# Two hybrid layers on one core: eight modulation columns moved out of the attention, and VectorE copies one head's transposes

## The chip, the core and the metric

The kernel runs on one core of one Trainium2 chip. The core has a matrix engine (TensorE, "PE" in the profile, its weight loads "PEld"), VectorE ("DVE"), ScalarE ("ACT"), GpSimd ("POOL") and SyncE ("SP"), which here only issues loads. Matrix results land in PSUM, eight banks of 2 KB per partition; everything else is in SBUF. The metric is the time of one execution on the device in microseconds; the number quoted is the median of the runs.

## The reference, cut to what matters

Two layers run over 128 context tokens and 512 latent tokens of width 1024. The part of a layer that this change touches:

```python
def _modulation(cond, ada_w, ada_b):          # 6 x 1024 = 48 columns of 128 outputs
    m = jax.nn.silu(cond) @ ada_w + ada_b
    return jnp.split(m[:, None, :], 6, axis=-1)

def _layer(x, cond, mixer, ...):
    sh1, sc1, ga1, sh2, sc2, ga2 = _modulation(cond, ada_w, ada_b)
    h = _rmsnorm(x, g_pre_mix) * (1.0 + sc1) + sh1
    mixed, side = mixer(_split_proj(h, w_in))      # retention heads beside attention heads
    x = x + ga1 * _rmsnorm(mixed @ w_out, g_post_mix)
    h = _rmsnorm(x, g_pre_ffn) * (1.0 + sc2) + sh2
    x = x + ga2 * _rmsnorm(_conv_ffn(h, w_up, conv_w, conv_b, w_down), g_post_ffn)
```

The attention heads of the latent tokens (8 heads, a neighbourhood window with a bias, and 128 cached context keys) do per block of 128 queries: scores, plus bias, row maximum, exponential, row sum, and the product with the values. Only `ga1, sh2, sc2, ga2`, which are needed after the mixer, are modulation columns that this change moves.

## The kernel before, in words

All products are float32 made of three passes with operands split in a high and a low part. A weight tile of 128 x 1024 arrives by DMA in `raw`, a ring of four slots; ScalarE writes its high part to `w_hi` (split_hi, L778) and VectorE the rest to `w_lo` (split_lo, L1354), which also frees the slot. `w_hi` and `w_lo` are rings of four tiles too: tile g is split as soon as the matrix engine is done with tile g-4.

One stream of tiles per layer feeds the ring. Its order is written out by hand in `ORDER`: "w" is a weight tile, "a" a modulation column, which is also a tile of 128 x 1024. VectorE alone works a column: `ada_first` (L1365) multiplies it with the first condition vector and sums, `ada_second` (L1371) does so with the second, and only that one frees the slot. `stream_ada` and `stream_in` give the place of a tile in the stream. SyncE issues a load as soon as the slot it needs is free, strictly in stream order.

VectorE's order is the order of its code, and each engine works strictly in order. Columns 16 to 47 ("column 0" of the stream below is number 16) are scattered between the weight tiles. The input projection has seven blocks of four tiles: weight tiles 0 to 19 are blocks 0 to 4, done token tile by token tile; 20 to 27 are blocks 5 and 6, done column by column, with `kq_evac` on ScalarE turning the results into keys and queries. The retention heads run in between: `chunk_state`, `decay_queries`, `weigh_scores` and `centre` on VectorE prepare what the matrix engine takes next (`retention_block`, `retention`). Tiles 28 to 35 are the output projection.

The attention is a loop of 20 units (`PAIRS`: four head pairs with four query blocks each, then four units for the context tokens), each with two heads e = 0, 1. It is a pipeline over steps i, written out for four engines:

- PE, step i: `na_scores(i)` into banks 0 and 1 or 2 and 3; `na_transposes(i-1)`, the exponentials of head e to bank `NA_T[e]`, which is 4 or 5; `na_values(i-2)`; after every fourth unit `na_outputs`, the reciprocal row sums spread over the rows. Steps 1 to 4 also hold `mix_transposes` of the retention result.
- DVE, step i: `na_weigh(i)` (L1600, bias and maximum; L1596 for the context units), `mix_low` in steps 2 to 5, `split_lo(31)` in step 5, then from step 5 to 20 one half of a modulation column, then for a finished group the reciprocal, a copy of the result out of PSUM (L1891), one step later the product (L1895) and after it the low part (L1904).
- ACT, step i: for e = 0, 1: `exponentials(i, e)` (L1158), then `copy_transposed(i-1, e)` (L1166), which takes the transposed exponentials from bank 4 or 5 to `pt`.

The semaphores between them: `na_s` scores done, `na_m` maximum done, `na_e` exponential done, `na_t` transposed, `na_p` copied, `na_av` values done. `na_transposes(u)` waits for the exponential and for the copy that empties its bank; `na_values(u)` waits for both copies of the unit.

Of the kernel before, what the change touches and what calls it, by code (L numbers as in the profile page):

```python
# [24 lines left out]
P = 128  # L25
# [70 lines left out]

ORDER = ("wwww" "wwww" "waawaaww" "wwaawwaa" "wwww" "wwawawaaa" "wwaawaawwaawww" "aaaaaaaa" "waawaawaw")
W_POS = [i for i, kind in enumerate(ORDER) if kind == "w"]
# [69 lines left out]
def build(nc, t):  # L168
    with ExitStack() as ctx:
# [204 lines left out]
        na_t = counted("na_t", 2 * NPU)  # L374
        na_p = counted("na_p", 2 * NPU)
        na_av = counted("na_av", NPU)
# [388 lines left out]
        def _(act):  # L765
# [324 lines left out]
            for layer in range(DEPTH):  # L1090
# [77 lines left out]
                for i in range(NPU + 3):  # L1168
                    for e in range(2):
                        if i < NPU:  # L1170
                            exponentials(i, e)
                        if 1 <= i < NPU + 1:
                            copy_transposed(i - 1, e)
                    if i == 0:
# [174 lines left out]
        def _(dve):  # L1349
# [183 lines left out]
            def retention_block(layer):  # L1533

                split_lo(16, layer)
                chunk_state(1, layer)
                split_lo(17, layer)
                decay_queries(0, layer)
                chunk_state(2, layer)
                split_lo(18, layer)  # L1540
                chunk_state(3, layer)
                weigh_scores(0, layer)
                decay_queries(1, layer)
                split_lo(19, layer)
                weigh_scores(1, layer)

            def retention(layer):

                for c in range(3):
                    split_lo(20 + c, layer)  # L1550
                    centre(c, layer)
                    weigh_scores(c + 2, layer)
                    if c < 2:
                        decay_queries(c + 2, layer)
                    if c:
                        ada(ADA_FIRST + 7 + c, layer)
                split_lo(23, layer)
                centre(3, layer)
                for col in range(ADA_FIRST + 10, ADA_FIRST + 13):
                    ada(col, layer)  # L1560
# [24 lines left out]
            def na_weigh(i, layer):  # L1585
# [7 lines left out]
                for e in range(2):  # L1593
# [4 lines left out]
                    else:  # L1598
                        c0 = keys_of(jb)[0]
                        dve.tensor_tensor_reduce(sp[:, i % 2, e, 0:n], src[:, 0:n], bias[:, 2 * g + e, c0:c0 + n],  # L1600
                                                 -1.0, BIG, ALU.add, ALU.min, nmax[:, i % 2, e:e + 1]).then_inc(na_m, 1)

            def group_sums(layer):
# [224 lines left out]
            for layer in range(DEPTH):  # L1828
# [25 lines left out]

                for q in (0, 2):
                    split_lo(12 + q, layer)
                    split_lo(13 + q, layer)
                    ada(ADA_FIRST + q + 4, layer)
                    ada(ADA_FIRST + q + 5, layer)
                retention_block(layer)  # L1860
# [3 lines left out]
                for g in range(26, 31):  # L1864
                    if g in (26, 27, 29):
                        col = ADA_FIRST + 13 + 2 * (g - 26 - g // 29)
                        ada(col, layer)
# [5 lines left out]
                for i in range(NPU + 3):  # L1873
# [4 lines left out]
                    if i == 5:  # L1878
                        split_lo(31, layer)
                    if 5 <= i < 21:  # L1880
                        (ada_first if i % 2 else ada_second)(ADA_FIRST + 19 + (i - 5) // 2, layer)
                    if i == 14:
# [201 lines left out]
        def _(pe):  # L2084
# [289 lines left out]
            def na_transposes(u, layer):  # L2374
                for e in range(2):
                    pe.wait_ge(na_e, at(na_e, layer, 2 * u + e + 1))
                    if u >= 1:
                        pe.wait_ge(na_p, at(na_p, layer, 2 * u - 1 + e))
                    for i, (c0, p0, n, tile) in enumerate(spans_of(PAIRS[u])):
# [3 lines left out]
            def na_values(u, layer):  # L2383
                g, jb = PAIRS[u]
                pe.wait_ge(na_p, at(na_p, layer, 2 * u + 2))
                if jb == 0 and g >= 2:
# [405 lines left out]
```

## Time and profile before

| what | value |
|---|---|
| median of 3 runs | 1602.45 us (1602.03 to 1604.36) |
| span of the profiled execution | 1601.0 us |
| PE busy | 1575.8 us, 98% |
| DVE busy | 1275.6 us, 80% |
| ACT busy | 794.1 us, 50% |
| POOL busy | 379.2 us, 24% |
| attention loop of layer 0 / layer 1 | about 264 to 316 us / 1045 to 1096 us |

The profiled execution has no time of its own in the list of runs; its span is 1.45 us under their median. Busy times of PE are modelled, and a stretched instruction counts as busy.

### The profile page before, as it was taken

What the parts mean: (1) busy time and instruction counts of PE and PEld (TensorE: products, weight loads), DVE (VectorE), ACT (ScalarE), POOL (GpSimd) and SP (SyncE); (2) the same over time, 40 slices, a digit from 0 to 9 for tenths busy, and PEclk for the clock granted to TensorE, in tenths of its full rate; (3) what the DMA queues carried; (4) which work ended last, traced back from release to release, by engine and by line L of the source; (5) the groups of instructions that cost most, each with busy time, mean ns of one, the idle gap of its engine ahead of it and who ended that gap; (6) DMA issues with size and microseconds to landing.
All of it is one profiled execution on the core that took longest, in us unless ns stands there. A gap on an engine that the chain in (4) does not pass through costs nothing.

```text
span 1601.0 us, 28310 instructions
## 1 busy us (share of the span) xinstructions
PE 1575.8 (98%) x9688; PEld 1389.2 (87%) x9688; DVE 1275.6 (80%) x2255; ACT 794.1 (50%) x1483; POOL 379.2 (24%) x302
## 2 busy tenths in 40 slices
PE   8999999999999999999999999999999999999998
PEld 6788898689999999888878889967899999998886
DVE  7876677968999999966669556987689999998575
ACT  5433235638655565533383323274766565563333
POOL 0031033001455455200000400700035455541000
PEclk9999999999999999999999999999999999999999
DMA  9343265361222222454414414736312222335451
GB/s 369 122 132 111 74 222 179 95 168 55 66 81 89 79 92 79 148 168 158 152 40 145 138 54 134 260 107 146 79 64 82 80 91 79 92 92 178 125 184 66
DMA packets 65494, 195.04 MB, mean 122 GB/s; under 512 B 15361, under 2 KB 16769, under 8 KB 65153
## 3 DMA queue, kind: packets, MB, share of 16 engines
q1 hardware_dynamic: 50114, 175.54, 35.1%
q10 hardware_dynamic: 15296, 18.39, 3.5%
q8 instruction: 53, 0.87, 0.3%
q14 instruction: 31, 0.25, 0.1%
HBM read 187.05 MB, written 6.85 MB: 121 GB/s over the span
## 4 chain that ended last, share of the span: by engine, by line
PE 84%; DVE 7%; issue 2%; ACT 2%; DMA 1%; ACTq 1%; DVEq 0%; SPq 0%
PE bank L2087 14%; PE bank L2088 13%; PE bank L2089 13%; PE bank L2597 10%; PE bank L2599 10%; PE bank L2598 10%; DMA raw<-in_stream 1%; PE bank L2393 1%; PE bank L2457 1%; PE bank L2455 1%; PE bank L2453 1%; PE bank L2380 1%; PE bank L2109 1%; DVE w_lo L1354 1%; PE bank L2277 1%
## 5 line engine op out<-in xcount | busy, mean ns | idle before, releaser
L778 ACT ACTIVATE w_hi<-raw 128x1024 fp32r<-128x1024 f32 (+1 forms) x120 | 123.1, 1029 | 389.0 <-PE bank L2089 325.1
L1354 DVE TENSOR_TENSOR w_lo<-raw,w_hi 128x1024 fp32r<-128x1024 f32 (+1 forms) x128 | 156.3, 1228 | 162.4 <-ACT w_hi L778 162.2
L2087 PE MATMUL bank<-w_hi,aT_lo 128*128 128x512 f32 x520 | 210.5, 405 | 2.1 <-DVE aT_lo L1787 2.0
L2088 PE MATMUL bank<-w_lo,aT_hi 128*128 128x512 f32 x520 | 206.0, 396 | 0.0
L2089 PE MATMUL bank<-w_hi,aT_hi 128*128 128x512 f32 x520 | 205.6, 395 | 0.0
L2597 PE MATMUL bank<-aT_hi,w_lo 128*128 128x322 f32 x640 | 199.8, 312 | 4.5 <-DVE u L1953 4.5
L2598 PE MATMUL bank<-aT_lo,w_hi 128*128 128x322 f32 x640 | 199.4, 312 | 0.0
L2599 PE MATMUL bank<-aT_hi,w_hi 128*128 128x322 f32 x640 | 198.6, 310 | 0.0
L1252 ACT ACTIVATE w_hi<-raw 128x512 fp32r<-128x512 f32 x200 | 117.8, 627 | 105.8 <-POOL raw L660 105.8
L2087 PE MATMUL bank<-w_hi,m_lo 128*128 128x512 f32 x400 | 158.5, 396 | 0.0
L2088 PE MATMUL bank<-w_lo,m_hi 128*128 128x512 f32 x400 | 157.3, 393 | 0.0
L2089 PE MATMUL bank<-w_hi,m_hi 128*128 128x512 f32 x400 | 157.2, 393 | 0.0
L1942 DVE TENSOR_TENSOR w_lo<-raw,w_hi 128x512 fp32r<-128x512 f32 x200 | 140.7, 734 | 0.0
L2597 PEld LDWEIGHTS bank<-aT_hi,w_lo 128*128 128x128 f32 x640 | 120.7, 189 | 6.0 <-DVE u L1953 5.0
L2598 PEld LDWEIGHTS bank<-aT_lo,w_hi 128*128 128x128 f32 x640 | 121.3, 190 | 0.0
L2599 PEld LDWEIGHTS bank<-aT_hi,w_hi 128*128 128x128 f32 x640 | 121.3, 190 | 0.0
L2087 PEld LDWEIGHTS bank<-w_hi,aT_lo 128*128 128x128 f32 x520 | 98.2, 189 | 26.5 <-DVE aT_lo L1787 3.4
L2089 PEld LDWEIGHTS bank<-w_hi,aT_hi 128*128 128x128 f32 x520 | 98.4, 189 | 23.3
L2088 PEld LDWEIGHTS bank<-w_lo,aT_hi 128*128 128x128 f32 x520 | 98.4, 189 | 20.8
L649 POOL TENSOR_TENSOR raw<-raw 128x512 f32<-128x512 f32 x40 | 52.6, 1316 | 258.6 <-DVE bank L1983 137.4
L639 POOL TENSOR_TENSOR bias<-bias,masks 128x192 f32<-128x192 f32 (+1 forms) x48 | 59.1, 1269 | 198.0 <-DMA bias<-in_bias 198.0
L2599 PE MATMUL bank<-s_hi,w_hi 128*128 128x322 f32 x320 | 99.8, 312 | 0.0
(287 smaller groups left out, 3865.9 us busy)
## 6 DMA issues: line engine op xcount, KB each, us to landing
raw<-in_stream SPq DMA_DIRECT2D x304, 512.0 KB, 3.6
lead<-in_lead SPq DMA_DIRECT2D x16, 512.0 KB, 10.6
bias<-in_bias ACTq DMA_DIRECT2D x8, 896.0 KB, 10.3
na_v<-vn ACTq DMA_DIRECT2D x2, 1280.0 KB, 5.6
x<-in_xs SPq DMA_DIRECT2D x4, 512.0 KB, 12.4
vt<-na_v ACTq DMA_DIRECT2D x16, 128.0 KB
gb_mix<-gates ACTq DMA_DIRECT2D x2, 1024.0 KB, 6.2
gb_ffn<-gates ACTq DMA_DIRECT2D x8, 256.0 KB, 4.5
```

What stands on the lines that cost most here:

```text
L639: i_ = pool.tensor_tensor(part, part, masks[:, m0 * CG:(m0 + n) * CG].rearrange("p (g c) -> p g c", c=CG).unsqueeze(2) .to_broadcast([P, n ...
L649: pool.tensor_tensor(g_, g_, a_, ALU.subtract).then_inc(t1_done, 1)
L778: act.activation(w_hi[:, g % 4, 0:n], raw[:, s % 4, 0:n], ACT.Copy).then_inc(hi_done, 1)
L1252: act.activation(block_of(w_hi, n), block_source(n, e), ACT.Copy).then_inc(blk_hi, 1)
L1354: dve.tensor_tensor(w_lo[:, g % 4, 0:n], raw[:, s % 4, 0:n], w_hi[:, g % 4, 0:n].bitcast(F32), ALU.subtract).then_inc(raw_free[s % 4], 1)
L1942: i_ = dve.tensor_tensor(block_of(w_lo, n), block_source(n, e), block_of(w_hi, n).bitcast(F32), ALU.subtract)
L2087: pe.matmul(out, ll, rh, start=start, stop=False)
L2088: pe.matmul(out, lh, rl, start=False, stop=False)
L2089: return pe.matmul(out, lh, rh, start=False, stop=stop)
L2597: pe.matmul(out, wl, rhs_hi[:, k, :], start=k == 0, stop=False)
L2598: pe.matmul(out, wh, rhs_lo[:, k, :], start=False, stop=False)
L2599: i_ = pe.matmul(out, wh, rhs_hi[:, k, :], start=False, stop=k == HP - 1)
```

## The change

Three parts.

1. `ORDER`: the eight columns that stood together behind tile 31 ("aaaaaaaa") are gone from there, and every column moves forward. The stretch for block 3 (tiles 12 to 15) has eight columns instead of four, one column stands behind tile 16, two ahead of tile 20, and one more ahead of tile 23. Every tile from 24 to 31 stands exactly eight places later than before.
2. VectorE's code follows: after each of tiles 12 to 15 two columns; column 12 in `retention_block`; columns 13 and 14 at the start of `retention`; column 17 ahead of tile 23. In the attention loop no column is left.
3. ScalarE's loop keeps `copy_transposed` for e = 0 only. VectorE gets a function of the same name for e = 1, called in step i behind `na_weigh(i)`, `mix_low` and `split_lo(31)` and ahead of the group's reciprocal. It counts on a new semaphore `na_q`; `na_transposes` of head 1 waits for `na_q` in place of `na_p`, and `na_values` waits for both.

```diff
@@ -94,7 +94,7 @@
 
 
 
-ORDER = ("wwww" "wwww" "waawaaww" "wwaawwaa" "wwww" "wwawawaaa" "wwaawaawwaawww" "aaaaaaaa" "waawaawaw")
+ORDER = ("wwww" "wwww" "waawaaww" "waawaawaawaa" "wawwwaa" "wwawaawaaa" "wwaawaawwaawww" "waawaawaw")
 W_POS = [i for i, kind in enumerate(ORDER) if kind == "w"]
 A_POS = [i for i, kind in enumerate(ORDER) if kind == "a"]
 assert len(W_POS) == G_IN + G_OUT and len(A_POS) == ADA - ADA_FIRST
@@ -372,7 +372,8 @@
         na_m = counted("na_m", 2 * NPU)
         na_e = counted("na_e", 2 * NPU)
         na_t = counted("na_t", 2 * NPU)
-        na_p = counted("na_p", 2 * NPU)
+        na_p = counted("na_p", NPU)
+        na_q = counted("na_q", NPU)
         na_av = counted("na_av", NPU)
         na_r = counted("na_r", GROUPS)
         na_c = counted("na_c", GROUPS)
@@ -1166,11 +1167,12 @@
                     act.activation(pt[:, u % 2, e, 0:n], bank[NA_T[e]][:, 0:n], ACT.Copy).then_inc(na_p, 1)
 
                 for i in range(NPU + 3):
-                    for e in range(2):
-                        if i < NPU:
-                            exponentials(i, e)
-                        if 1 <= i < NPU + 1:
-                            copy_transposed(i - 1, e)
+                    if i < NPU:
+                        exponentials(i, 0)
+                    if 1 <= i < NPU + 1:
+                        copy_transposed(i - 1, 0)
+                    if i < NPU:
+                        exponentials(i, 1)
                     if i == 0:
                         kq_evac(NB_IN - 1, 3, layer)
                     if 1 <= i <= 4:
@@ -1534,6 +1536,7 @@
 
                 split_lo(16, layer)
                 chunk_state(1, layer)
+                ada(ADA_FIRST + 12, layer)
                 split_lo(17, layer)
                 decay_queries(0, layer)
                 chunk_state(2, layer)
@@ -1546,6 +1549,8 @@
 
             def retention(layer):
 
+                ada(ADA_FIRST + 13, layer)
+                ada(ADA_FIRST + 14, layer)
                 for c in range(3):
                     split_lo(20 + c, layer)
                     centre(c, layer)
@@ -1553,10 +1558,11 @@
                     if c < 2:
                         decay_queries(c + 2, layer)
                     if c:
-                        ada(ADA_FIRST + 7 + c, layer)
+                        ada(ADA_FIRST + 14 + c, layer)
+                ada(ADA_FIRST + 17, layer)
                 split_lo(23, layer)
                 centre(3, layer)
-                for col in range(ADA_FIRST + 10, ADA_FIRST + 13):
+                for col in range(ADA_FIRST + 18, ADA_FIRST + 21):
                     ada(col, layer)
                 centre(NC, layer)
                 group_sums(layer)
@@ -1599,6 +1605,13 @@
                         c0 = keys_of(jb)[0]
                         dve.tensor_tensor_reduce(sp[:, i % 2, e, 0:n], src[:, 0:n], bias[:, 2 * g + e, c0:c0 + n],
                                                  -1.0, BIG, ALU.add, ALU.min, nmax[:, i % 2, e:e + 1]).then_inc(na_m, 1)
+
+            def copy_transposed(u, layer):
+                n = P * len(spans_of(PAIRS[u]))
+                dve.wait_ge(na_t, at(na_t, layer, 2 * u + 2))
+                if u >= 2:
+                    dve.wait_ge(na_av, at(na_av, layer, u - 1))
+                dve.tensor_copy(pt[:, u % 2, 1, 0:n], bank[NA_T[1]][:, 0:n]).then_inc(na_q, 1)
 
             def group_sums(layer):
 
@@ -1852,18 +1865,17 @@
                 rotate(1, range(NT), layer)
                 split_lo(11, layer)
 
-                for q in (0, 2):
+                for q in range(4):
                     split_lo(12 + q, layer)
-                    split_lo(13 + q, layer)
-                    ada(ADA_FIRST + q + 4, layer)
-                    ada(ADA_FIRST + q + 5, layer)
+                    ada(ADA_FIRST + 2 * q + 4, layer)
+                    ada(ADA_FIRST + 2 * q + 5, layer)
                 retention_block(layer)
                 retention(layer)
                 split_lo(25, layer)
                 group_norm(layer)
                 for g in range(26, 31):
                     if g in (26, 27, 29):
-                        col = ADA_FIRST + 13 + 2 * (g - 26 - g // 29)
+                        col = ADA_FIRST + 21 + 2 * (g - 26 - g // 29)
                         ada(col, layer)
                         ada(col + 1, layer)
                     split_lo(g, layer)
@@ -1877,8 +1889,8 @@
                         mix_low((0, 1) if i == 2 else (i - 1,), layer)
                     if i == 5:
                         split_lo(31, layer)
-                    if 5 <= i < 21:
-                        (ada_first if i % 2 else ada_second)(ADA_FIRST + 19 + (i - 5) // 2, layer)
+                    if 1 <= i < NPU + 1:
+                        copy_transposed(i - 1, layer)
                     if i == 14:
                         dve.wait_ge(*freed(stream_ada(ADA_MIX - 1), layer))
                         times_gain(4 * KD, C_GF, 1.0, layer).then_inc(mod_done, 1)
@@ -2375,14 +2387,16 @@
                 for e in range(2):
                     pe.wait_ge(na_e, at(na_e, layer, 2 * u + e + 1))
                     if u >= 1:
-                        pe.wait_ge(na_p, at(na_p, layer, 2 * u - 1 + e))
+                        copied = na_q if e else na_p
+                        pe.wait_ge(copied, at(copied, layer, u))
                     for i, (c0, p0, n, tile) in enumerate(spans_of(PAIRS[u])):
                         i_ = pe.transpose(bank[NA_T[e]][:, i * P:(i + 1) * P], sp[:, u % 2, e, c0 - p0:c0 - p0 + P], ident[:])
                     i_.then_inc(na_t, 1)
 
             def na_values(u, layer):
                 g, jb = PAIRS[u]
-                pe.wait_ge(na_p, at(na_p, layer, 2 * u + 2))
+                pe.wait_ge(na_p, at(na_p, layer, u + 1))
+                pe.wait_ge(na_q, at(na_q, layer, u + 1))
                 if jb == 0 and g >= 2:
                     pe.wait_ge(na_n, at(na_n, layer, g - 1))
                 spans = spans_of(PAIRS[u])
```

VectorE in layer 0 from the split of tile 16 to that of tile 18 (L1354; `ada_first` is L1365, `ada_second` L1371, states L1514 and L1519, decayed queries L1501). Before:

```order
L1354 TENSOR_TENSOR w_lo<-raw,w_hi 128x1024
L1514 TENSOR_TENSOR sst<-st0,cdec 64x512 x2
L1519 TENSOR_TENSOR sst<-bank1,sst 64x512 x2
L1354 TENSOR_TENSOR w_lo<-raw,w_hi 128x1024
L1501 TENSOR_TENSOR qf<-qT,qexp 64x4x128 x4
L1514 TENSOR_TENSOR sst<-sst,cdec 64x512 x2
L1519 TENSOR_TENSOR sst<-bank2,sst 64x512 x2
```

After (every line number from here on is two or more higher):

```order
L1356 TENSOR_TENSOR w_lo<-raw,w_hi 128x1024
L1516 TENSOR_TENSOR sst<-st0,cdec 64x512 x2
L1521 TENSOR_TENSOR sst<-bank1,sst 64x512 x2
L1367 ISA ada_sq,mod<-raw,cond,par 128x1024
L1367 ISA mod 128x1
L1373 ISA raw,mod<-raw,cond,par 128x1024
L1373 ISA mod 128x1
L1356 TENSOR_TENSOR w_lo<-raw,w_hi 128x1024
L1503 TENSOR_TENSOR qf<-qT,qexp 64x4x128 x4
L1516 TENSOR_TENSOR sst<-sst,cdec 64x512 x2
L1521 TENSOR_TENSOR sst<-bank2,sst 64x512 x2
```

Column 12 now stands between the first state and tile 17.

VectorE in the attention loop from the end of step 5 to step 7 (L1354 splits tile 31, L1889 and L1891 are the reciprocal and the copy of the first group, L1600 `na_weigh`, L1895 the product). Before:

```order
L1354 TENSOR_TENSOR w_lo<-raw,w_hi 128x1024
L1365 ISA ada_sq,mod<-raw,cond,par 128x1024
L1365 ISA mod 128x1
L1889 RECIPROCAL rec<-esum 128x8
L1891 COPY nao<-bank6 128x512
L1600 ISA sp,nmax<-bank0,bias 128x384
L1600 ISA nmax 128x1
L1600 ISA sp,nmax<-bank1,bias 128x384
L1600 ISA nmax 128x1
L1371 ISA raw,mod<-raw,cond,par 128x1024
L1371 ISA mod 128x1
L1895 TENSOR_TENSOR nao<-nao,bank6 128x512
```

After (L1614 is the new copy, L1606 `na_weigh`, L1903 the group's copy, L1907 the product):

```order
L1356 TENSOR_TENSOR w_lo<-raw,w_hi 128x1024
L1614 COPY pt<-bank5 128x384
L1901 RECIPROCAL rec<-esum 128x8
L1903 COPY nao<-bank6 128x512
L1606 ISA sp,nmax<-bank0,bias 128x384
L1606 ISA nmax 128x1
L1606 ISA sp,nmax<-bank1,bias 128x384
L1606 ISA nmax 128x1
L1614 COPY pt<-bank5 128x384
L1907 TENSOR_TENSOR nao<-nao,bank6 128x512
```

Each half of a column has gone, and a copy from bank 5 stands ahead of the group's work.

The matrix engine in step 5, transposes of unit 4 and values of unit 3 (L2380, L2393), with what each waits for. Before:

```order
L2380 MATMUL bank4<-ident,sp 128x128 [waits na_p,na_e]
L2380 MATMUL bank4<-ident,sp 128x128 x2
L2380 MATMUL bank5<-ident,sp 128x128 [waits na_p,na_e]
L2380 MATMUL bank5<-ident,sp 128x128 x2
L2393 MATMUL bank6<-pt,ctx_v 64x128 [waits na_p]
L2393 MATMUL bank6<-pt,ctx_v 64x128
L2393 MATMUL bank6<-pt,vt 64x128 x4
```

After (L2393 and L2407):

```order
L2393 MATMUL bank4<-ident,sp 128x128 [waits na_p,na_e]
L2393 MATMUL bank4<-ident,sp 128x128 x2
L2393 MATMUL bank5<-ident,sp 128x128 [waits na_q,na_e]
L2393 MATMUL bank5<-ident,sp 128x128 x2
L2407 MATMUL bank6<-pt,ctx_v 64x128 [waits na_q,na_p]
L2407 MATMUL bank6<-pt,ctx_v 64x128
L2407 MATMUL bank6<-pt,vt 64x128 x4
```

The order is the same; the values' first product waits for two semaphores instead of one.

## Rows read from the trace of the kernel before

**Rows 1.** Page, part 1: busy time, share and instructions of each engine.

```profile
PE 1575.8 (98%) x9688; PEld 1389.2 (87%) x9688; DVE 1275.6 (80%) x2255; ACT 794.1 (50%) x1483; POOL 379.2 (24%) x302
```

**Rows 2.** Stretches: us, busy (x instructions) of PE, PEld, DVE, ACT, POOL; PEclk, DMA share, GB/s.

```profile
101.50:133.00 31.50, 31.50 (x157) 25.54 (x158) 16.86 (x20) 13.04 (x24) 19.38 (x12) 1.00 0.40 122
...
168.00:200.00 32.00, 32.00 (x258) 26.33 (x254) 22.14 (x34) 7.70 (x11) 0.00 (x0) 1.00 0.25 74
...
279.00:316.00 37.00, 35.90 (x387) 25.53 (x386) 36.07 (x95) 26.80 (x86) 0.00 (x0) 1.00 0.36 101
...
1058.00:1096.00 38.00, 36.90 (x400) 26.16 (x398) 37.07 (x97) 27.92 (x88) 0.00 (x0) 1.00 0.32 98
```

**Rows 3.** Waits, attention of layer 0 (262 to 316): us, times, longest.

```profile
PE bank L2393 <- DVE aT_lo L1582: 1.0, 1, 1.0
...
PE bank L2380 <- ACT pt L1166: 0.5, 2, 0.3
...
PE bank L2404 <- DVE nao L1891: 0.4, 1, 0.4
...
PEld bank L2393 <- issue: 4.0, 24, 0.2
```

**Rows 4.** Order of time, PE, attention: start, us, engine, instruction, [idle before <- releaser].

```profile
276.39 0.49 PE L2369 MATMUL bank<-ctx_kT,qT 64*128 64x128 f32 x4
...
288.70 0.49 PE L2369 MATMUL bank<-ctx_kT,qT 64*128 64x128 f32 x4
...
295.61 0.87 PE L2380 MATMUL bank<-ident,sp 128*128 128x128 f32 x6
...
299.63 0.49 PE L2369 MATMUL bank<-ctx_kT,qT 64*128 64x128 f32 x4
...
300.49 1.03 PE L2380 MATMUL bank<-ident,sp 128*128 128x128 f32 x6
...
308.68 0.55 PE L2380 MATMUL bank<-ident,sp 128*128 128x128 f32 x3
...
309.41 0.52 PE L2380 MATMUL bank<-ident,sp 128*128 128x128 f32 x3 [0.19 <-ACT pt L1166]
...
311.09 0.66 PE L2380 MATMUL bank<-ident,sp 128*128 128x128 f32 x2
...
313.06 0.44 PE L2380 MATMUL bank<-ident,sp 128*128 128x128 f32 x2
```

**Rows 5.** Order of time, DVE, steps 5 and 6 of the loop.

```profile
278.96 1.21 DVE L1354 TENSOR_TENSOR w_lo<-raw,w_hi 128x1024 fp32r<-128x1024 f32 x1
...
280.09 1.28 DVE L1365 CUSTOM_DVE_ANT_0 ada_sq<-raw,cond,par 128x1024 f32<-128x1024 f32 x1
...
281.41 0.64 DVE L1891 COPY nao<-bank 128x512 f32<-128x512 f32 x1
...
281.96 0.54 DVE L1600 CUSTOM_DVE_ANT_0 sp<-bank,bias 128x384 f32<-128x384 f32 x1
```

**Rows 6.** Groups by line, DVE, 279 to 316: busy us, mean ns.

```profile
L1365 DVE CUSTOM_DVE_ANT_0 ada_sq<-raw,cond,par 128x1024 f32<-128x1024 f32 x7 | 8.9, 1278 | 0.0
...
L1596 DVE TENSOR_REDUCE nmax<-bank 128x1 f32<-128x128 f32 x8 | 1.9, 282 | 0.1
```

**Rows 7.** Order of time, DVE, input blocks and ahead of the attention.

```profile
111.66 2.10 DVE L1354 TENSOR_TENSOR w_lo<-raw,w_hi 128x1024 fp32r<-128x1024 f32 x1 [6.09 <-ACT w_hi L778]
...
143.06 1.22 DVE L1354 TENSOR_TENSOR w_lo<-raw,w_hi 128x1024 fp32r<-128x1024 f32 x1 [5.23 <-ACT w_hi L778]
...
168.83 1.23 DVE L1354 TENSOR_TENSOR w_lo<-raw,w_hi 128x1024 fp32r<-128x1024 f32 x1 [5.42 <-ACT w_hi L778]
...
202.79 1.23 DVE L1354 TENSOR_TENSOR w_lo<-raw,w_hi 128x1024 fp32r<-128x1024 f32 x1 [5.15 <-ACT w_hi L778]
...
234.69 1.62 DVE L1365 CUSTOM_DVE_ANT_0 ada_sq<-raw,cond,par 128x1024 f32<-128x1024 f32 x1
```

**Rows 8.** Order of time, POOL, during block 2.

```profile
118.83 6.04 POOL L612 TENSOR_TENSOR tm<-tm,kdec 128x512 f32<-128x512 f32 x5 [6.16 <-PE bank L2200]
```

## The prediction

> **What bounds the kernel now.** I read the page's busy times first. The matrix engine is busy for 98% of the span [rows 1], so a change elsewhere pays only where that engine waits or is stretched. Then the stretches. In the input blocks PE is busy for all of 31.50 and all of 32.00 us, while VectorE is busy for 16.86 and 22.14 [rows 2]. In the attention VectorE is busy for 36.07 of 37.00 us in layer 0 and 37.07 of 38.00 in layer 1, PE for 35.90 and 36.90 [rows 2]. So both engines are near their limit there, and nowhere else in the stretches that the change touches.
>
> The waits of PE in the attention of layer 0 come to little: 1.0 us for a low part of the retention result, 0.5 for ScalarE's copies, 0.4 for the group's copy on VectorE [rows 3]. But they are not all. A set of transposes whose second half waits is drawn as a longer instruction. The sequence in order of time shows this: six transposes take 0.87 us when nothing is late, 1.03 at 300.49, and from 308.68 to 309.93 (1.25) where their second head waits for ScalarE's copy [rows 4]. The two of a context unit take 0.44 or 0.66 [rows 4].
>
> How much is lost? Four steps form a group. From 288.70 to 299.63, the clean one, they take 10.93 us; from 276.39 to 288.70 they take 12.31 [rows 4]. That is 1.38 lost, and VectorE's rows say why: in step 5 it splits a tile (278.96), works half a column (280.09), copies the group (281.41) and begins the next maximum only at 281.96 [rows 5], 2 us after its scores (step 6 starts them about 276.39 + 2.62 = 279.01 and needs 0.85). The other places: 1.03 - 0.87 = 0.16, 1.25 - 0.87 = 0.38, 0.66 - 0.44 = 0.22 [rows 4], and I allow 0.1 for residues in the clean group. Together 2.2 us per layer. The 1.0 us ahead of it is another matter, below.
>
> **The change part by part.**
>
> *Columns out of the attention.* Sixteen halves per layer leave the loop, each 1.28 us and 0.08 for its sum, of which 0.07 overlaps: 16 x 1.28 = 20.5 us of VectorE, one in every step from 5 to 20 [rows 6].
>
> *The second head's copy to VectorE.* The trace has no copy of 384 elements from PSUM on VectorE. From below the reduction over 128 gives 0.28 us [rows 6], from above the copy of 512 gives 0.64 [rows 5]. A straight line between them gives 0.28 + 256 x 0.36/384 = 0.52 for 384, which I take. Per layer 16 of 0.52 and 4 of 0.28 are 9.4 us. By the Trainium skill, "VectorE: DVE Perf Modes", on the TRN2 errata, such a copy is 120 + 384 cycles at 0.96 GHz, an estimate of 0.53 us, which changes nothing in the sum; no row here shows it.
>
> So VectorE's work in the loop falls by about 11 us per layer, and a step costs it two maxima of 0.54 at most (starts 281.96 and, by the same row, half a microsecond later) and one copy, 1.6 us, plus 0.6 to 0.7 of group work in three steps of four. A step of PE takes 10.93/4 = 2.7 us. VectorE is no longer the bound, and PE should run every group at the clean pace. The new copy of unit i-1 stands behind the maximum of unit i. In a clean step it ends about 0.95 + 1.05 + 0.5 = 2.5 us after the step's scores begin (0.95 to the first maximum), and PE asks for it at the second half of the next transposes, about 2.4 + 0.75 + 0.4 = 3.5 us after. Margin 1 us. ScalarE sheds the same 20 copies and has no new wait.
>
> *One new lateness.* In step 5 the copy stands behind `mix_low` and the split of tile 31, in front of the group's copy. The split ends at 280.09, where the half column begins [rows 5]. The copy ends at about 280.65; PE would reach the second half of unit 5's transposes at 279.01 + 0.85 + 0.40 = 280.26. It waits 0.4 us. Behind it, the group's copy ends at 281.2 instead of 281.41 + 0.64 = 282.05 and is in time. So 0.4 of the 2.2 comes back: 1.8 us per layer.
>
> *The 1.0 us at the start stays.* It waits for `mix_low`, which stands behind a maximum that waits for PE's own scores; no column is near, and the first copies on VectorE come while it waits for PE anyway. With it stays what the first four steps lose.
>
> *Columns into the input blocks.* A column costs two halves, 2.4 us where POOL is quiet. They fall in VectorE's own gaps, which are waits for ScalarE's high part, thus for PE. Two columns (4.9) go ahead of the split at 111.66, gap 6.09, and two ahead of that of tile 15, one block's rhythm later with an equal gap; one (2.4) ahead of 143.06, gap 5.23; two (4.9) ahead of 168.83, gap 5.42; one (2.4) ahead of 202.79, gap 5.15 [rows 7]. The tightest leaves 0.5 us. Even an overrun is covered: `w_lo` is a ring of four, so a split may come some three tiles late before PE misses it. Cost 0. If that cover were gone, each microsecond of overrun would be one on the path.
>
> *The loads.* SyncE's queue has the same tiles, earlier. The stretch from 101.5 to 133 carries twelve tiles instead of eight: its DMA share of 0.40 [rows 2] becomes an estimated 0.6. From tile 24 on all places move by eight, a multiple of the four slots, so the slot and the tile that frees it are as before. Cost 0.
>
> Here a rule of the skill speaks against the change. First the rows: half a column takes 1.62 us at 234.69 beside POOL's mask additions, 1.28 in the attention without POOL, and the split at 111.66 takes 2.10 against 1.22 [rows 6, 7]; POOL works 6.04 us from 118.83 [rows 8], where new columns now lie. The Trainium skill, "SBUF — State Buffer", on who interferes with whom, says that a VectorE instruction with two SBUF inputs and a GpSimd one that reads SBUF exclude each other wholly for a whole instruction. The trace agrees in direction, not in size. By the rule VectorE would lose up to 6 us there instead of 4 x 0.34 = 1.4 by the rows; either is less than the three tiles of cover, so the sum is the same.
>
> *The extra wait.* `na_values` waits for two semaphores, 20 times per layer. From below it costs nothing: the second three of the six transposes at 295.61 already wait for two, and the six run in one 0.87 [rows 4]. From above, the weight loads of the values stand idle for "issue" 4.0/24 = 0.17 us each [rows 3]; another such piece per unit would be 3.4 us per layer. I take 0, since the row with two waits is the nearer one. Queued behind it are only PE's own products.
>
> **Sum.** 2 x (2.2 - 0.4) = 3.6 us. The profiled span of 1601.0 becomes 1597.4; the median stands 1.45 above the span, and so goes from 1602.45 to 1598.9.
>
> **The rivals.**
>
> A. *Only part of it.* The copies on VectorE come late in more places than step 5, or the stretched transposes are PE's own; then the 0.4 of step 5 and its like take back most. For it: the group work and the copy stand in one queue. Against it: the margin of 1 us above. Gain 0 to 2.6, time about 1601.
>
> B. *The start shortens too.* ScalarE loses a copy ahead of its high parts in steps 1 to 4, and the 1.0 and its neighbours shrink. Against it: VectorE's maximum there waits for PE. Up to 2.2 + 1.4 per layer, 7.2 in all: 1596.5 if most comes, 1595.3 as the end.
>
> C. *The added wait costs, the slower side.* Every unit's values lose 0.17 us at the new second wait: + 40 x 0.17 = 6.8, less 3.6, gives 1605.7. It decides from 3.6/40 = 0.09 us per unit on. For it: the idle issue pieces. Against it: the transposes' two waits without a seam.
>
> D. *The input blocks pay.* A column overruns into `centre` or `chunk_state`, and PE, which is at 100% there, waits. Two to four microseconds in each layer would give about 1603. Against it: gaps and cover above.
>
> **How the numbers follow.** The forecast, a gain of 2.7 to 5 us, has 0.60; A 0.25; B 0.05; C 0.05; D 0.05. Its own range is 1597.4 to 1599.8. The range that should hold 8 in 10 takes in A down to no gain and most of B: 1596.3 to 1602.3. About 0.2% (3.2 us, below 1599.2) can be told from no change here. Of the forecast's 0.60 some 0.47 lies beyond that, with B's 0.05: 0.52 faster. C and D give 0.07 slower beyond the bound, the rest is within: 0.41.
>
> **What would show it.** Right: in the loop from step 5 VectorE busy about 65%; every group of four steps at 10.9 us; the step 16 transposes at 0.87; one wait of PE for the VectorE copy of about 0.4 us in step 6; the columns at 1.2 to 1.3 us per half in the former gaps and PE still fully busy from 101.5 to 200; attention of each layer about 1.8 us shorter, and everything behind it only shifted. Wrong: transposes or values that wait for the VectorE copy in many steps (A), a seam in front of each unit's values (C), PE waiting in blocks 3 to 5 (D).

## The result: 1609.97 us, slower by 0.38%

| kernel | median | range, runs | ratio to before, 95% interval |
|---|---|---|---|
| before, timed beside it | 1603.51 us | 1602.03 to 1605.7, 6 | |
| changed | 1609.97 us | 1607.23 to 1611.85, 6 | 1.0038 [1.0028, 1.0047] |

The forecast was 1598.9 with a range to 1602.3. The profiled execution took 1609.07 us, its span 1607.3, 6.3 more than before. First the page's busy times of the changed kernel, which answer to [rows 1]:

```profile
PE 1577.0 (98%) x9688; PEld 1391.8 (87%) x9688; DVE 1317.3 (82%) x2295; ACT 781.3 (49%) x1443; POOL 393.2 (24%) x302
```

VectorE works 42 us more than before and POOL 14 more. About 20 of the 42 are the 40 copies that ScalarE did before (L1614: 32 of 128x384 at 0.55 us, 8 of 128x128 at 0.28). No other work was added, so instructions of both engines were stretched. The stretches of [rows 2] in the changed kernel, and one between them; each row holds its length, then the busy time of PE, PEld, DVE, ACT and POOL, then the granted clock:

```profile
101.50:133.00 31.50, 31.50 (x154) 25.54 (x154) 30.26 (x26) 12.81 (x23) 26.16 (x12) 1.00 0.46 134
135.00:168.00 33.00, 30.43 (x200) 24.39 (x200) 29.09 (x42) 8.89 (x11) 0.00 (x0) 0.95 0.44 140
168.00:200.00 32.00, 32.00 (x249) 26.20 (x248) 24.74 (x39) 6.04 (x8) 0.00 (x0) 1.00 0.36 115
279.00:316.00 37.00, 36.41 (x399) 26.48 (x397) 27.95 (x85) 24.94 (x75) 0.00 (x0) 1.00 0.05 16
```

The attention gains what was forecast: PE works 36.41 of 37.00 us (35.90 before) and VectorE 27.95 (36.07 before). That is 76% for VectorE, where the forecast had 65%, still far from the limit. The input blocks are not as forecast: VectorE is busy for 30.26 of 31.50 us (16.86 before), and in the next 33 us, where PE had no gap before, it is short of 2.57 us and the clock is at 0.95. Three rows of PE's waits, over the whole execution:

```profile
PE bank L2289 <- DVE sst L1521: 5.1, 2, 2.6
...
PE bank L2407 <- DVE aT_lo L1588: 1.9, 2, 1.0
...
PE bank L2393 <- DVE pt L1614: 0.7, 2, 0.4
```

The first is new: once per layer PE stops for 2.6 us in front of the first retention scores, because the second state of `chunk_state` is late. The second is the 1.0 us that was to stay, the third the 0.4 us that was to come.

Where the time went, by the start of the same instruction in both traces:

| PE's instruction | before | changed | difference |
|---|---|---|---|
| last increments ahead of the first retention scores | 150.04 | 150.16 | 0.12 |
| first retention scores | 151.12 | 153.88 | 2.76 |
| fourth product of the block behind them | 153.01 | 157.28 | 4.27 |
| scores of step 5 of the attention | 276.39 | 280.85 | 4.46 |
| first product behind the attention | 315.83 | 318.49 | 2.66 |

So a layer first loses 4.46 us and then gains 1.80. Layer 1 repeats it: its first retention scores wait 2.57 us at 937.40 and the clock takes 1.6 more behind them. At the scores of step 5 of its attention (1064.19 against 1056.69) the difference is 7.50, at the first product behind the attention (1101.83 against 1096.13) it is 5.70, so here too 1.80 come back. At the last product it is 6.27: most of the rest is one new wait of 0.48 us for a low part of a weight tile in the feed-forward part of layer 1, at 1202.99. Seven of the nine experiments below have this wait too (0.44 to 0.90), the kernel before has not; so not everything behind the attention was only shifted; its cause stays open.

**VectorE ahead of the stop.** The columns of the fourth input block, in order of time (start, duration; the short rows that read a column's sum are left out):

```profile
105.62 2.06 DVE L1367 CUSTOM_DVE_ANT_0 ada_sq<-raw,cond,par 128x1024 f32<-128x1024 f32 x1
...
107.61 2.91 DVE L1373 CUSTOM_DVE_ANT_0 raw<-raw,cond,par 128x1024 f32<-128x1024 f32 x1
...
113.30 3.42 DVE L1373 CUSTOM_DVE_ANT_0 raw<-raw,cond,par 128x1024 f32<-128x1024 f32 x1
...
117.79 1.27 DVE L1367 CUSTOM_DVE_ANT_0 ada_sq<-raw,cond,par 128x1024 f32<-128x1024 f32 x1
...
118.99 2.08 DVE L1373 CUSTOM_DVE_ANT_0 raw<-raw,cond,par 128x1024 f32<-128x1024 f32 x1
...
133.51 1.27 DVE L1373 CUSTOM_DVE_ANT_0 raw<-raw,cond,par 128x1024 f32<-128x1024 f32 x1
...
152.43 1.39 DVE L1521 TENSOR_TENSOR sst<-bank,sst 64x512 f32<-64x512 f32 x2
```

And POOL in the same stretch:

```profile
106.56 2.88 POOL L607 TENSOR_TENSOR dtab<-dist,lg 128x1024 f32<-128x1024 f32 x1
...
112.37 3.26 POOL L627 TENSOR_TENSOR dtab<-dtab,pr 128x1024 f32<-128x1024 f32 x1
118.95 8.98 POOL L613 TENSOR_TENSOR tm<-tm,kdec 128x512 f32<-128x512 f32 x5 [3.32 <-PE bank L2212]
127.90 3.39 POOL L633 TENSOR_TENSOR dtab<-dtab,ident 128x1024 f32<-128x1024 f32 x1
```

Nine of the sixteen halves lie beside POOL and take 2.06, 2.91, 2.92, 3.42, 2.08, 2.05, 2.05, 2.06 and 3.42 us, together 22.97; the others take 1.27 or 1.28. That is 11.5 us more than 9 x 1.27: 6.2 of it beside POOL's rows from 106.56 to 115.6, 3.2 beside the five decayed keys from 118.95, 2.2 beside the row at 127.90. POOL pays too: 8.98 for the five decayed keys against 6.04 [rows 8], 2.88 for exponents that took 1.90 before. VectorE has no gap from 103.95 to 161.8, and the state that PE wants is finished at 153.8 instead of 149.8. Before, VectorE waited 19.1 us in all between the split at 103.83 and that state; the five columns that were put there are about 12 us in quiet and would have fitted. The 11.5 us on top did not.

The Trainium skill, "SBUF — State Buffer", on who interferes with whom, says that a VectorE instruction with two SBUF inputs contends with a GpSimd one that reads SBUF, and that the port pair they share is an exclusive lock; it names the whole instruction as the time for which the lock is held (of VectorE's two-port modes). Whole turns beside the decayed keys would be 1.27 + 6.04/5 = 2.48 us; the rows show 2.05. Beside the exponents they would be 1.27 + 1.90 = 3.17; the rows show 2.91. The trace agrees to within a fifth; both sums are estimates.

**PE behind the stop.**

```profile
153.88 2.08 PE L2289 MATMUL bank<-qT,kT 64*128 64x128 f32 x16 [2.57 <-DVE sst L1521]
155.89 0.79 PE L2099 MATMUL bank<-w_hi,aT_lo 128*128 128x512 f32 x1
156.48 0.63 PE L2100 MATMUL bank<-w_lo,aT_hi 128*128 128x512 f32 x1
156.91 0.53 PE L2101 MATMUL bank<-w_hi,aT_hi 128*128 128x512 f32 x1
157.28 0.40 PE L2099 MATMUL bank<-w_hi,aT_lo 128*128 128x512 f32 x1
```

The stretch from 153 to 156 and the next, by the view of stretches:

```profile
153.00:156.00 3.00, 2.12 (x17) 1.90 (x17) 2.94 (x5) 0.00 (x0) 0.00 (x0) 0.63 0.00 0
156.00:159.00 3.00, 3.00 (x11) 2.45 (x12) 2.92 (x5) 0.60 (x1) 0.00 (x0) 0.80 0.54 175
```

Before, the same scores took 1.16 us and the three products 0.50, 0.39 and 0.39. After the idle 2.57 us PE ran for 3.1 us, from 153.88 to 157.0, at the lower of its two clock levels, 1.2 GHz (granted clock 0.50). The difference grows from 2.76 to 4.27, so the clock adds 1.5 us to this stop. In layer 1 the scores behind the stop still take 1.16 us; the products from 938.83 to 942.2 are the slow ones, 0.6 us each, and cost 1.6.

### The profile page after: what moved, and what is told of

Same layout as the page of the kernel before. It is cut to its first block, busy times and chain, and to the rows that moved or that the text cites. A ratio compares the mean times of both kernels' runs of the same rounds, so it can differ in the third digit from the quotient of the medians.

```text
span 1607.3 us, 28340 instructions
## 1 busy us (share of the span) xinstructions
PE 1577.0 (98%) x9688; PEld 1391.8 (87%) x9688; DVE 1317.3 (82%) x2295; ACT 781.3 (49%) x1443; POOL 393.2 (24%) x302
## 4 chain that ended last, share of the span: by engine, by line
PE 80%; DVE 10%; issue 4%; DMA 1%; ACT 1%; ACTq 1%; DVEq 0%; SPq 0%
PE bank L2099 12%; PE bank L2100 12%; PE bank L2101 12%; PE bank L2611 10%; PE bank L2613 10%; PE bank L2612 10%; DVE ada_sq L1367 2%; PE bank L2407 2%; DVE w_lo L1356 1%; DMA raw<-in_stream 1%; PE bank L2393 1%; PE bank L2471 1%; PE bank L2469 1%; PE bank L2467 1%; PE bank L2121 1%
```

## The experiments

Each was timed beside the kernel before, whose median was 1603.74 us beside the first four, 1603.60 beside the next three and 1604.24 beside the last two.

**1. The same columns in other gaps.** The fourth block as before; the eight columns in VectorE's waits behind POOL's work. `ORDER` and the column numbers in `retention_block` and `retention` follow and are left out here.

```diff
-                for q in range(4):
+                for q in (0, 2):
                     split_lo(12 + q, layer)
-                    ada(ADA_FIRST + 2 * q + 4, layer)
-                    ada(ADA_FIRST + 2 * q + 5, layer)
+                    split_lo(13 + q, layer)
+                    ada(ADA_FIRST + q + 4, layer)
+                    ada(ADA_FIRST + q + 5, layer)
...
                 for c in range(3):
                     split_lo(20 + c, layer)
...
-                    if c:
-                        ada(ADA_FIRST + 14 + c, layer)
-                ada(ADA_FIRST + 17, layer)
+                    ada(ADA_FIRST + 11 + c, layer)
+                ada(ADA_FIRST + 14, layer)
+                ada(ADA_FIRST + 15, layer)
                 split_lo(23, layer)
+                ada(ADA_FIRST + 16, layer)
+                ada(ADA_FIRST + 17, layer)
```

> The attention and the copy are those of the changed kernel. The fourth input block has four columns again, as before; the eight moved columns lie in VectorE's waits behind POOL's work: one ahead of the split of tile 17, two ahead of that of tile 20, one in each of the three retention turns, and the rest round the split of tile 23. Theory (columns run beside POOL's SBUF work, are stretched by it, and push chunk_state(2) behind the time at which PE wants it): no wait of PE for sst beyond 0.3 us, no fall of the granted clock behind it, attention 1.8 us shorter per layer as in the changed kernel, time 1603.5 - 3.6 = 1599.9. Rival 'sheer number' (eight more columns anywhere in the input blocks and the retention cost PE): PE waits move to a later place, time 1605 to 1610. Rival 'the copy or its second wait costs outside what I read': still above 1603.5.

Measured: 1600.69 us, ratio 0.9978 [0.9969, 0.9987], 3.05 less than before and some 9 less than the changed kernel. PE has no wait for `sst`, and from 135 to 168 no gap and no fall of the clock:

```profile
135.00:168.00 33.00, 33.00 (x224) 26.32 (x224) 26.75 (x39) 7.59 (x10) 0.00 (x0) 1.00 0.34 108
```

PE begins the first scores of the attention at 254.11 (254.19 before). The columns' number in the projection is harmless, their place was not.

**2. One SBUF input instead of two**, with the changed kernel's places.

```diff
+                if ADA_FIRST + 4 <= col < ADA_FIRST + 12:
+                    dve.tensor_reduce(mod[:, col, 0:1], raw[:, s % 4, :], AX.X, ALU.add).then_inc(ada_part, 1)
+                    return
                 dve.tensor_tensor_reduce((ada_junk if col < ADA_FIRST else ada_sq)[:], raw[:, s % 4, :], ...
```

and the same in `ada_second`.

> The changed kernel, but the halves of the eight columns in the fourth input block are plain sums over the same 1024 elements (one SBUF input instead of two), so these columns' products with the condition are left out. Order, tiles and waits are the same. Theory (an instruction of VectorE with two SBUF inputs and one of POOL shut each other out): the halves take 1.1 to 1.3 us each beside POOL too, POOL's rows are back near 1.9 and 6 us, VectorE ends chunk_state(2) near 150, PE's wait for sst goes from 2.6 us to under 0.3, time 1609.97 - 2 x 4.2 = 1601.5, down to 1600. Rival 'any traffic of VectorE on SBUF is slowed beside POOL': halves stay at 2 us and more, time stays 1609 to 1610. Rival 'number of columns': the same stretch is as full, time stays.

Measured: 1601.22 us, ratio 0.9982 [0.9973, 0.9991]. First VectorE, then POOL:

```profile
104.68 1.21 DVE L1368 TENSOR_REDUCE mod<-raw 128x1 f32<-128x1024 f32 x1
105.81 1.21 DVE L1377 TENSOR_REDUCE mod<-raw 128x1 f32<-128x1024 f32 x1
...
120.06 1.21 DVE L1368 TENSOR_REDUCE mod<-raw 128x1 f32<-128x1024 f32 x1
...
147.61 1.39 DVE L1527 TENSOR_TENSOR sst<-bank,sst 64x512 f32<-64x512 f32 x2
```

```profile
105.62 1.90 POOL L607 TENSOR_TENSOR dtab<-dist,lg 128x1024 f32<-128x1024 f32 x1
...
118.01 6.03 POOL L613 TENSOR_TENSOR tm<-tm,kdec 128x512 f32<-128x512 f32 x5 [6.15 <-PE bank L2218]
```

All sixteen halves take 1.20 or 1.21, beside POOL or not, and POOL is back at 1.90 and 6.03. The splits, which still have two SBUF inputs, still show the stretch (2.10 at 110.84). The state is finished at 149.0 and the stop is gone. The elements read from `raw` and the loads are the same. But a plain sum differs in more than the second input: it writes no full-width result to SBUF, and it needs no short instruction to read the sum (32 instructions of 0.08 us fewer). So this run alone leaves the write as a rival. Rows of the kernel before, in its feed-forward part, speak against it:

```profile
1208.01 0.54 DVE L1928 SCALAR_TENSOR_TENSOR cvg<-bank,par,cvg 128x321 f32<-128x321 f32 x1
1208.46 0.54 DVE L1931 SCALAR_TENSOR_TENSOR cvg<-bank,par,cvg 128x320 f32<-128x320 f32 x1
1208.92 1.42 DVE L1942 TENSOR_TENSOR w_lo<-raw,w_hi 128x512 fp32r<-128x512 f32 x1
```

```profile
1208.21 1.58 POOL L669 TENSOR_TENSOR m<-m,cvg 128x642 f32 x1
```

All three VectorE instructions overlap POOL's work and write their full width to SBUF. The first two read one wide operand from SBUF and one from PSUM, and take the 0.54 us that they take in quiet; of L1928's instructions of this form 36 lie beside POOL, at 0.54 or 0.55. The third reads both from SBUF and takes 1.42 in place of 0.68. So it is the second SBUF input that stretches.

**3. Both copies on ScalarE**, the columns as in the changed kernel: `copy_transposed(i - 1, e)` stands behind `exponentials(i, e)` on ScalarE again, and VectorE has none.

> The changed kernel with both heads' copies on ScalarE, as before: the columns' move alone. Theory: the loss of 4.46 us per layer ahead of the attention is the columns' alone and stays; in the attention VectorE has room, and what ScalarE's copies cost before (0.38 in step 16, 0.5 of waits) stays, so its gain is 1.2 to 2.2 us per layer: time between 1609.2 and 1611.2. Rival 'the copy on VectorE is what costs': time falls to below 1606.

Measured: 1608.39 us (1604.39 to 1612.12), ratio 1.0025 [1.0012, 1.0038]; a little under the range expected, and its interval overlaps that of the changed kernel. So most of the loss at least belongs to the columns, and moving the copy back does not cure it. The profiled execution shows the two parts of the stop apart. In layer 0:

```profile
153.53 1.16 PE L2286 MATMUL bank<-qT,kT 64*128 64x128 f32 x16 [2.56 <-DVE sst L1520]
```

The same wait as in the changed kernel, but the scores behind it keep their 1.16 us and the difference to before stays at 2.4. In layer 1 of the same execution it is 5.17 at the scores and 6.74 a few products later. So the stop does not always cost clock. In this profile layer 1 also lost 3 us in the first steps of its attention: ScalarE's high part of a tile, which came late (1051.00, behind a wait of 1.65 for the load), stands ahead of an exponential for which PE waits 1.83 us. No experiment tests this.

**4. Only the copy moved**, columns left in the attention. Against the kernel before, besides the copy's own code on the three engines:

```diff
+                    if 1 <= i < NPU + 1:
+                        copy_transposed(i - 1, layer)
                     if 5 <= i < 21:
                         (ada_first if i % 2 else ada_second)(ADA_FIRST + 19 + (i - 5) // 2, layer)
```

> The kernel before with the second head's copy on VectorE and the columns left in the attention: the copy's move alone. VectorE is busy for 36.07 of 37.00 us of the attention already, and the copies add 9.4 us per layer, so it becomes the bound: the loop is some 8 us longer per layer, 1603.5 + 16 = 1619.5, with PE waiting for the copies in most steps from 5 on, and nothing changes ahead of the attention. Rival 'ScalarE's copies were the bound': faster than 1603.5. Rival 'VectorE's idle time hides the copies': 1603 to 1606.

Measured: 1610.51 us, ratio 1.0048 [1.0035, 1.0061], and PE has no new wait ahead of the attention. VectorE is the bound there, as expected, but I had put twice the price:

```profile
279.00:316.00 37.00, 33.07 (x348) 23.04 (x349) 36.97 (x97) 19.98 (x63) 0.00 (x0) 1.00 0.29 89
```

Of the 9.4 us of copies per layer only about 4.3 reach PE (from the scores of step 2 to the last outputs 62.79 us against 58.45): VectorE still had waits to fill at both ends of the loop (before, it was busy for 47.06 of the 59 us from 265 to 324, now for 53.51).

**5. Experiment 1 with both copies on ScalarE.**

> The columns in VectorE's gaps as in the first experiment, both heads' copies back on ScalarE: the columns' move alone, without the input blocks' loss. Theory (the attention gains nearly all of its time from the columns' leaving; the copy on VectorE adds a few tenths): layer 0's loop ran 1.25 us shorter with both copies on ScalarE and 1.4 with one on VectorE, so time 1603.74 - 2.5 = 1601.2, within 1 us of the first experiment. Rival 'the copy carries the gain': time back at 1603 to 1604.

Measured: 1599.84 us, ratio 0.9976 [0.9966, 0.9987], the same as experiment 1. From the scores of step 2 to the last outputs of layer 0 it takes 56.68 us; experiment 1 takes 56.69. From step 2 on, the whole gain of the attention is the columns'. Ahead of that, layer 1 of this profile lost 2.5 us between steps 1 and 2, behind a late tile as in experiment 3 (PE waits 1.87 at 1044.07); by the medians experiment 5 is no slower than experiment 1.

**6. One column later.** The changed kernel, with a single column carried past `chunk_state(2)`; in `ORDER` it moves one place back, behind the next tile.

```diff
                 chunk_state(1, layer)
-                ada(ADA_FIRST + 12, layer)
                 split_lo(17, layer)
                 decay_queries(0, layer)
                 chunk_state(2, layer)
+                ada(ADA_FIRST + 12, layer)
                 split_lo(18, layer)
```

> The changed kernel with one column (2.4 us) taken from in front of chunk_state(2) and put behind it; everything else, the twelve columns beside POOL too, as in the changed kernel. Theory (VectorE's queue ahead of chunk_state(2) is 2.6 us too long, and the rest of the loss is the granted clock that falls after PE's stop): PE's wait for sst goes from 2.6 us to 0.2 or none, the clock stays at 1.00 behind it, and the loss of 4.1 us per layer goes to 0.3; time 1610 - 7.5 = 1602.5, down to 1601 if nothing else is late. Rival 'the delay only moves to chunk_state(3) and the weighed scores': PE waits 2 us one step later, time 1606 to 1610. Rival 'VectorE's contention with POOL slows PE's work in another way': the time hardly moves.

Measured: 1601.16 us, ratio 0.9979 [0.9968, 0.9989]. A move of 2.4 us of VectorE's work in each layer takes 8.8 us off the changed kernel's median. The stop and the stretch in which the clock had fallen:

```profile
150.21 1.16 PE L2289 MATMUL bank<-qT,kT 64*128 64x128 f32 x16 [0.16 <-DVE sst L1521]
```

```profile
153.00:156.00 3.00, 3.00 (x14) 2.43 (x13) 2.94 (x5) 1.41 (x3) 0.00 (x0) 1.00 0.70 199
```

POOL is as stretched as in the changed kernel, and PE does not pay for it:

```profile
117.69 8.98 POOL L613 TENSOR_TENSOR tm<-tm,kdec 128x512 f32<-128x512 f32 x5 [3.32 <-PE bank L2212]
```

VectorE is still busy for 32.41 of the 33 us from 135 to 168, and the states and weighed scores behind the column are in time. What decides is what stands ahead of `chunk_state(2)` in the queue.

**7. Two exchanges in the attention**, on top of experiment 1.

```diff
+                    if i == 2:
+                        mix_low((0,), layer)
                     if 1 <= i < NPU:
                         na_weigh(i, layer)
                     if 2 <= i <= 5:
-                        mix_low((0, 1) if i == 2 else (i - 1,), layer)
-                    if i == 5:
-                        split_lo(31, layer)
+                        mix_low((i - 1,), layer)
                     if 1 <= i < NPU + 1:
                         copy_transposed(i - 1, layer)
+                    if i == 5:
+                        split_lo(31, layer)
```

> The first experiment's kernel with two exchanges in VectorE's order in the attention: in step 2 the low part of the first mixed tile goes ahead of the maximum, and in step 5 the copy goes ahead of the split of tile 31. Theory (PE's two waits there, 0.97 for aT_lo and 0.38 for pt, are this in-order queue's): both waits go, 1.3 us per layer, time 1600.7 - 2.7 = 1598.0. Rival 'they are replaced by a wait for the exponentials of step 2, which come 0.7 us later': 0.4 to 0.8 us per layer is left, 1599.5.

Measured: 1598.08 us, ratio 0.9965 [0.9951, 0.9979], the fastest kernel of this study, 12 us under the changed one. Both waits are gone; the second mixed tile now waits longer in their place. All of PE's waits from 254 to 320:

```profile
PE bank L2363 <- DVE aT_lo L1590: 0.8, 2, 0.6
PE bank L2363 <- ACT qT L902: 0.2, 1, 0.2
```

So per layer 0.8 us are gained in the trace (55.88 against 56.69), not 1.3: 0.26 from step 2 to step 5 and 0.55 behind it.

**8. Experiment 7 with both copies on ScalarE.** With VectorE's copy the exchange of step 5 falls away too.

> The last kernel (columns in the gaps, the first mixed tile's low part ahead of the maximum in step 2) with both heads' copies on ScalarE. Theory (with the columns gone the copy on VectorE is worth nothing that can be measured): within 1 us of the last kernel's 1598.1, thus 1597.5 to 1599.1, with at most 0.2 us of waits for ScalarE's pt per layer. Rival 'the copy on VectorE frees ScalarE for the exponentials': 1600 or more, with PE waiting for sp or pt in several steps.

Measured: 1600.43 us, ratio 0.9984 [0.9976, 0.9993]. Outside what I expected. The two intervals just overlap, but the traces differ by 0.93 us per layer (56.81 against 55.88), part of it here:

```profile
266.21 0.80 PE L2409 MATMUL bank<-pt,vt 64*64 64x128 f32 x8 [0.43 <-DVE aT_lo L1589]
```

ScalarE makes the high part of the mixed tile behind its copies, so the low part can't come early. Of the 0.93 us 0.40 lie between steps 2 and 5 and 0.53 behind them. By experiments 1 and 5 the copy on VectorE was worth nothing; with the two exchanges of experiment 7 it is worth this.

**9. The exchange of step 2 alone, in the kernel before.**

> The kernel before with only the exchange in step 2 (the first mixed tile's low part ahead of the maximum): columns and copies as before. Theory (PE's 0.97 us wait for aT_lo is VectorE's in-order queue, and does not depend on the columns): that wait goes, 0.97 less per layer, less 0.3 for the second tile's wait; time 1603.6 - 1.3 to 1.9 = 1602.0. Rival 'VectorE, full from step 5 on, gives the gain back there': 1603.6.

Measured: 1603.46 us, ratio 0.9997 [0.9988, 1.0007]: no change. From step 2 to the last outputs it takes 58.60 us against 58.45. The rival had the time right but not the place: from step 5 on the loop takes 47.91 us against 47.90, and the gain was gone before. PE still waits 0.43 for the first low part (267.76), as in experiment 8 with ScalarE's copies ahead of the high part, and then 0.62 for the second tile's (269.40), together more than the 0.97 that went.

## Why the prediction was wrong

- *Columns out of the attention, the copy's duration, the extra wait:* right. The copy of 384 took 0.55 us (0.52 forecast), a group of four steps 10.83 (287.51 to 298.34; 10.9 forecast), the transposes of step 16 0.87, PE's new wait in step 6 0.37 (0.4 forecast), and no seam stood in front of the values. The sum of 1.8 us per layer is what the trace shows, in both layers. VectorE's share, 76% in place of 65%, was a miss without effect. But I had put the gain to both edits; by experiments 1 and 5 the copy gave none of it.
- *"Columns into the input blocks ... Cost 0":* this step failed, at 4.3 us per layer. Its first fault is the price, "2.4 us where POOL is quiet". The block's columns lie beside POOL's work from 105.6 to 131 and cost 11.5 us more than in quiet. I had looked only at POOL's work from 118.83 and priced it at 4 x 0.34 = 1.4; the halves there lost 3.2, and the other 8.4 were lost beside rows of POOL that the prediction doesn't price. The 0.34 came from the row at 234.69, beside additions of 192 elements, and I carried it over to instructions of 512 and 1024; the split at 111.66, which I had named in the same sentence at 2.10 against 1.22, was the nearer row and gives 4 x 0.88 = 3.5. The rule of the Trainium skill, "up to 6 us there", was a little nearer than 1.4: with the split at 124.98 VectorE lost 4.0 there. Experiment 2 shows this fault alone: without the contention even these places are free.
- *"Even an overrun is covered: w_lo is a ring of four":* the second fault. The ring covers the splits. But the same queue holds `chunk_state(2)`, whose result PE takes directly. It was finished 1.3 us before PE began the scores (149.8 and 151.12), and that was all the cover. Experiment 6 shows it: 2.4 us less in front of it, and the stop is 0.16.
- *"If that cover were gone, each microsecond of overrun would be one on the path":* the third fault. The state came 4.0 us later than before; less 1.3 of cover, and less 0.1 by which PE itself came later, the stop is 2.6. The clock then makes it about 4.2 in either layer, though not in every execution (experiment 3).
- *Rival D* named the right mechanism and place (`chunk_state`), at 0.05 and with 2 to 4 us per layer for about 1603. By the prediction's own terms that sum should have been 1602.9 to 1606.9. The loss was 4.3 to 4.5, and it was set against a gain of 1.8 that was real.
- *The loads:* the slots of the ring came free late with the columns, ScalarE waited up to 8.86 us for a tile at 138.84, and that cost PE nothing. "Cost 0" was off by 0.2 us per layer elsewhere: at the start of the attention a tile came later, and the exponential behind its high part kept PE waiting 0.50 in place of 0.29 (267.95). That is the step from 4.27 to 4.46. The DMA share of 101.5 to 133 became 0.46, not 0.6.
- *Rivals A and B* did not come: no later copy but that of step 5, and the first steps were not shorter.

Not settled: which part of the spread between runs is the clock. Every kernel here stops PE for 2.2 to 2.3 us once per layer in the feed-forward part, waiting for VectorE's tile `u`, and behind 12 of these 22 stops the granted clock fell too, in the profile of the kernel before behind one of two. So two profiles can differ by such falls without any cause in the change. The six runs of the changed kernel have a mean granted clock of 0.994 to 0.997, the eight of experiment 6 0.997 to 0.999, which agrees with a fall behind each stop, but a run's mean doesn't say where it fell.

## What to carry to other kernels

Before work is put into an engine's gaps, list what stands behind it in that engine's queue and find the item whose result the bounding engine takes soonest; its slack is the budget, not the slack of the buffers in between. Price the work by what runs beside it: here an instruction of VectorE with two SBUF inputs took 1.6 to 2.7 times as long beside POOL's instructions of 512 and 1024 elements, and one with a single input took its normal time. If a large gap is needed and the engine's total fits, try the order before the amount: one column carried behind one state decided between 0.4% slower and 0.2% faster.

## What the runs showed of the hardware

- Column halves (two SBUF inputs, 1024 elements) beside POOL's instructions of 512 and 1024 elements: 2.05 to 3.42 us instead of 1.27; POOL's instructions beside them 1.4 to 1.5 times as long (8.98 against 6.04 us, 2.88 against 1.90). Reductions with one SBUF input over the same elements: 1.20 or 1.21 beside POOL and in quiet, with POOL at 1.90 and 6.03. Instructions with one wide input from PSUM and one from SBUF, with a full-width result in SBUF: 0.54 or 0.55 beside POOL, 0.54 in quiet.
- A stop of PE of 2.57 us was followed by a fall of the granted clock that cost about 1.5 us, in three of the four stops of this length in the profiles of the changed kernel and of experiment 3. Behind the fourth it stayed at 1.00. Of the stops of 2.2 to 2.3 us for `u`, two in each of the eleven profiles, 12 of 22 were followed by a fall, and both of the stops of 1.83 and 1.87 us in experiments 3 and 5 were. In each the clock was back at 1.00 within 6 us of the restart.
- A copy of 128x384 from PSUM on VectorE: 0.55 us; on ScalarE 0.47.
